# Attention heads in a new order of steps, and the differential layer's weight panels split by ScalarE and VectorE

## The chip, the cores and the metric

The kernel runs on one core of a Trainium2 chip. The metric is the time of one execution in microseconds (us), the median of three runs. TensorE (PE in the rows) multiplies, VectorE (DVE) reduces and works by element, ScalarE (ACT) evaluates functions and copies, GpSimd (POOL) works by element too, and SyncE (SP) issues most of the DMAs. The engines run side by side, each through its own list in order, and meet at semaphores.

## The reference, cut to what matters

One step of a trunk of four layers over 128 context tokens and 512 latent tokens (T = 640) of width 1024. Each layer is a modulated norm, a token mixer, a residual, a modulated norm, a SwiGLU FFN and a residual. The mixers are latent attention (MLA), differential attention, grouped-query attention with rotary positions, and a gated recurrence. The change touches the three attention mixers, of 8 heads each:

```python
def blocked_attention(q, k, v):          # per block of 128 queries
    sc = einsum('bqhgd,bkhd->bhgqk', qblk, k) * scale
    p = softmax(sc, axis=-1)
    return einsum('bhgqk,bkhd->bqhgd', p, v)

# differential: two softmaxes of 64-wide halves of q and k, one value
o = o1 - lam_full * o2
o = rmsnorm(o, g_sub) * (1.0 - lambda_init)
```

The query and the key of a head are projections of the layer's input, normed by their root mean square over the head's width and, for latent tokens, turned by rotary angles. In MLA a key is 128 values of its own beside 64 rotary values that all heads share (`kr`). In the differential layer they are 128 wide, two components of 64.

## The kernel before, in words

Everything lies transposed in SBUF: features on partitions, tokens along the free axis. A projection multiplies a 128-column panel of weights with all 640 tokens. To keep float32's precision each operand is split in a high and a low part, and `products` sums three products (high with high, high with low, low with high) over the panel's 8 tiles of 128 rows: 48 matmuls of 320 columns. Splitting a panel is two instructions over 128x1024: `w_hi` is a rounded copy of `raw`, `w_lo` is the difference. In the dense phases (output projections and FFN) ScalarE makes `w_hi` (`high_part`) and VectorE `w_lo` (`low_part`); in all others, the heads' projections among them, GpSimd does both. SyncE loads `raw` into three slots.

A head has two streams of work. The attention of head h goes over t = 0 to 4, blocks of 128 queries (4 of latent, 1 of context): scores (TensorE, float32 matmuls into banks psA and psB in turn), maximum (VectorE, L414, L418), exponential (ScalarE, L376), division (VectorE, `probs`, L422 to L429), five 128x128 transposes through psC (TensorE, L353, `turned`), a copy out of psC (ScalarE, L383, L385, `pt`), and at the end one product with the values (`pe_output`, L361). The preparation of head h + 1 is its projections into psD, evacuation (`evq`, `evk`: L395, L396), the sum of squares over partitions by a matmul with a matrix of ones (`ssq`, `ssk`: L312), the reciprocal root by a logarithm and an exponential (`rsq`, `rsk`: L400, L402), the norm (L434), a rotation by a matmul (`rotq`, `rotk`: L966, L976), the rotary sum (L438 to L441), and the transposes of the values. In the lists a step of the one stream stands between steps of the other. These orders are written out by hand in `head`, once for each of the three engines, and semaphores count marks in the same order (`pipelined_names` and the lists handed to `pipeline`). A list entry that waits holds up all behind it on its engine.

All preparation steps of one head, sums, rotations and value transposes included, use the one psum pair psD, so a projection cannot start before the last of them has been read. In the differential layer GpSimd splits three panels a head.

## Time and profile before

| | us |
|---|---|
| median of 3 runs (lowest, highest) | 3837.23 (3836.21, 3839.26) |
| the profiled execution | 3834.61 |
| its span | 3832.8 |
| TensorE busy in the span | 3417.5 (89%) |
| VectorE, ScalarE, GpSimd busy | 1907.0, 1093.3, 325.1 |
| granted TensorE clock, mean | 0.940 of full |

The chain of work that ended last is TensorE's for 78% of the span, ScalarE's for 8%, VectorE's for 6%. A timeline row gives the start, the length from the first start to the last end of a run of like instructions, and in brackets how long the engine sat idle before it and whose result ended the wait. TensorE's matmuls overlap: in a stream of 320-column products two start every 0.29 us though each row ends later, so lengths on TensorE are read from start to start. Full clock is 1.0.

### The profile page before, as it was taken

Reading aid. Unit: us, or ns where it says so; the run is one execution under the profiler, and the core shown is the slowest. Engines: PE = TensorE matmul, PEld = TensorE weight load, DVE = VectorE, ACT = ScalarE, POOL = GpSimd, SP = SyncE. Lnnn points to the kernel's source line nnn. Section 1 sums busy time; section 2 is a strip of 40 time slices with the busy share of each in tenths; the row PEclk is TensorE's granted clock in tenths of the full one; section 3 lists DMA queues with packets and bytes.
Section 4 is the critical chain, followed back from the end, with each engine's and each line's share of the span. In section 5 each row is a group of like instructions: output and inputs, shape, how many; then the busy total and the mean of one; then the engine's idle time right before and its main releaser. Section 6 shows DMA issues by size and latency. Waiting matters only on the chain.

```text
span 3832.8 us, 53039 instructions
## 1 busy us (share of the span) xinstructions
PE 3417.5 (89%) x20320; PEld 3050.3 (80%) x20320; DVE 1907.0 (50%) x2703; ACT 1093.3 (29%) x1710; POOL 325.1 (8%) x168
## 2 busy tenths in 40 slices
PE   7868888999987887789999878889999877799999
PEld 2645568999975666579999866589999877799999
DVE  2133345857353444458583534458573678633332
ACT  1324433211122333332111133332111255331111
POOL 0311100000012222000000021000000144000000
PEclk9979999999987888789999989999999988899999
DMA  7200003443221101025342210034442211122222
GB/s 264 90 14 12 17 23 112 147 156 123 75 69 32 32 27 32 3 76 182 124 155 72 71 38 18 17 99 159 137 143 71 66 52 41 55 66 77 72 76 77
DMA packets 421854, 304.02 MB, mean 79 GB/s; under 512 B 12019, under 2 KB 389494, under 8 KB 421622
## 3 DMA queue, kind: packets, MB, share of 16 engines
q1 hardware_dynamic: 411412, 293.23, 24.7%
q10 hardware_dynamic: 10338, 9.41, 0.7%
q8 instruction: 65, 1.06, 0.1%
q14 instruction: 39, 0.32, 0.0%
HBM read 298.49 MB, written 4.10 MB: 79 GB/s over the span
## 4 chain that ended last, share of the span: by engine, by line
PE 78%; ACT 8%; DVE 6%; DVEq 3%; issue 2%; ACTq 1%; DMA 1%; SPq 0%
PE psB L296 27%; PE psA L296 27%; PE psD L296 8%; PE psC L361 3%; PE psA L340 2%; PE psB L340 2%; ACT h_hi L1251 1%; PE psA L727 1%; ACT work L1248 1%; PE psD L312 1%; DVE work L2020 1%; PE psB L727 1%; PE psC L312 1%; ACT work L400 1%; ACT work L402 1%
## 5 line engine op out<-in xcount | busy, mean ns | idle before, releaser
L1269 ACT ACTIVATE w_hi<-raw 128x1024 fp32r<-128x1024 f32 (+1 forms) x304 | 314.2, 1035 | 1152.6 <-PE psB L296 762.1
L1734 DVE TENSOR_TENSOR w_lo<-raw,w_hi 128x1024 fp32r<-128x1024 f32 (+1 forms) x304 | 362.1, 1192 | 345.8 <-ACT w_hi L1269 345.4
L296 PE MATMUL psA<-h_hi,w_hi 128*128 128x320 f32 x1616 | 385.1, 320 | 71.8 <-DVE h_lo L1797 60.4
L697 POOL TENSOR_TENSOR w_hi<-raw,consts 128x1024 fp32r<-128x1024 f32 (+2 forms) x82 | 143.2, 1747 | 2916.1 <-PE psA L296 772.7
L296 PE MATMUL psA<-h_lo,w_hi 128*128 128x320 f32 x1616 | 377.0, 315 | 0.0
L296 PE MATMUL psA<-h_hi,w_lo 128*128 128x320 f32 x1616 | 376.6, 315 | 0.0
L296 PE MATMUL psB<-h_hi,w_hi 128*128 128x320 f32 x1616 | 368.7, 309 | 0.0
L296 PE MATMUL psB<-h_lo,w_hi 128*128 128x320 f32 x1616 | 368.6, 309 | 0.0
L296 PE MATMUL psB<-h_hi,w_lo 128*128 128x320 f32 x1616 | 368.6, 309 | 0.0
L296 PEld LDWEIGHTS psA<-h_hi,w_hi 128*128 128x128 f32 x1616 | 274.6, 193 | 92.2 <-issue 44.2
L1756 DVE SCALAR_TENSOR_TENSOR work<-work,silu_c 128x1024 f32<-128x1024 f32 x252 | 312.7, 1282 | 12.0 <-issue 0.5
L296 PEld LDWEIGHTS psA<-h_hi,w_lo 128*128 128x128 f32 x1616 | 278.6, 193 | 0.0
L296 PEld LDWEIGHTS psA<-h_lo,w_hi 128*128 128x128 f32 x1616 | 278.3, 193 | 0.0
L296 PEld LDWEIGHTS psB<-h_hi,w_hi 128*128 128x128 f32 x1616 | 270.8, 188 | 0.0
L296 PEld LDWEIGHTS psB<-h_lo,w_hi 128*128 128x128 f32 x1616 | 270.6, 188 | 0.0
L296 PEld LDWEIGHTS psB<-h_hi,w_lo 128*128 128x128 f32 x1616 | 270.4, 188 | 0.0
L296 PE MATMUL psA<-act_hi,w_hi 128*128 128x320 f32 x960 | 221.5, 312 | 18.4 <-DVE w_lo L1734 16.7
L296 PE MATMUL psA<-act_lo,w_hi 128*128 128x320 f32 x960 | 219.9, 310 | 0.0
L296 PE MATMUL psA<-act_hi,w_lo 128*128 128x320 f32 x960 | 219.8, 310 | 0.0
L296 PE MATMUL psD<-h_hi,w_hi 128*128 128x320 f32 (+1 forms) x672 | 181.1, 353 | 42.6 <-DVE work L441 15.6
L296 PE MATMUL psB<-act_hi,w_hi 128*128 128x320 f32 x960 | 218.8, 309 | 0.0
L296 PE MATMUL psB<-act_hi,w_lo 128*128 128x320 f32 x960 | 218.7, 309 | 0.0
(285 smaller groups left out, 5537.2 us busy)
## 6 DMA issues: line engine op xcount, KB each, us to landing
raw<-in_w_ffn_in SPq DMA_DIRECT2D x176, 512.0 KB, 3.9
work<-in_w_mod SPq DMA_DIRECT2D x144, 512.0 KB, 4.7
raw<-in_w_ffn_out SPq DMA_DIRECT2D x64, 512.0 KB, 3.7
work<-in_w_mod SPq DMA_DIRECT2D x12, 2048.0 KB, 8.1
raw<-in_w_ffn_out SPq DMA_DIRECT2D x32, 384.0 KB, 3.3
raw<-in_diff_w_in SPq DMA_DIRECT2D x24, 512.0 KB, 3.7
raw<-in_lru_w_in SPq DMA_DIRECT2D x16, 512.0 KB, 4.6
raw<-in_gqa_w_in SPq DMA_DIRECT2D x12, 512.0 KB, 3.7
```

Source lines behind the costliest of these rows:

```text
L296: last = nc.tensor.matmul(out[:, b, 0:half], w[slot][:, kt * cols + c0:kt * cols + c0 + P], r[:, o:o + half], start=(kt == 0 and p == 0), ...
L312: last = nc.tensor.matmul(out[:, b, 0:half], ones_, sq[:, b * half:(b + 1) * half], start=(k == 0), stop=(k == len(pieces) - 1))
L340: last = nc.tensor.matmul(s[:, b, 0:n], q[:, q0:q0 + P], k[:, k0:k0 + n], start=(m == 0), stop=(m == len(pairs[c]) - 1))
L361: nc.tensor.matmul(psC[:, 0, 0:NLAT], V[:, (k + 1) * P:(k + 2) * P], PT[:, k * NLAT:(k + 1) * NLAT], start=(k == 0), stop=(k == 4))
L400: nc.scalar.activation(halves(out, half), ps[:, :, 0:half], ACT.Ln, bias=eps, scale=1.0 / count)
L402: return nc.scalar.activation(out, out, ACT.Exp, scale=-0.5)
L697: nc.gpsimd.tensor_tensor(w_hi[s][:, 0:n], raw[s][:, 0:n], ones[:, 0:1].to_broadcast([P, n]), ALU.mult).then_inc(pool_hi, 1)
L727: last = nc.tensor.matmul(psum[q % 2][0:2, 0, :], silu_c[:, kt * 2:kt * 2 + 2], first_mod_w[q % 3][:, kt * 512:(kt + 1) * 512], start=(kt ...
L1248: nc.scalar.activation(s_, s_, ACT.Identity, bias=mod_col(layer, 3 * which, kt, cond), scale=gains[:, cond * KT + kt:cond * KT + kt + 1])
L1269: nc.scalar.activation(w_hi[s][:, 0:n], raw[s][:, 0:n], ACT.Copy).then_inc(hi_done, 1)
L1734: nc.vector.tensor_tensor(w_lo[s_][:, 0:n], raw[s_][:, 0:n], w_hi[s_][:, 0:n].bitcast(F32), ALU.subtract).then_inc(split_done, 1)
L1756: last = nc.vector.scalar_tensor_tensor(acc[cond], w_, c_, acc[cond], ALU.mult, ALU.add)
```

## The change

In all three attention mixers the hand-written lists are put in another order. In the two first mixers sums, rotations and value transposes go to psC, which the transposed probabilities use, and psD holds projections alone. A projection's 8 tiles are cut in pieces with steps of the attention between them, and waits are added so that psC's users follow one another. In the differential layer the end of a head (sum of squares of its output and its norm) moves into the next head. In MLA the rotary part of the score has all 128 rows (the shared key's first 64 are cleared, by one memset) instead of 64, and the loop over the two parts is outside the loop over banks. The maximum and the division of VectorE are separate steps, and the maxima come earlier. The differential layer becomes a dense phase for its panels: ScalarE makes `w_hi`, VectorE `w_lo`, two panels a head ahead for q and k and one head ahead for v, and those of its first head in the last turn of the FFN before it. GpSimd keeps the panels of MLA, grouped attention and the recurrence. The first two differential heads stand outside the loop.

The panel plan, the score loop, MLA's pairs, and TensorE's list of a differential head:

```diff
-            add("diff", HEADS, (2, 0, 1), [(KT, P)] * 3)
+            add("diff", HEADS, (2, 0, 1), [(KT, P)] * 3, True)
...
-                for b, k0, n in ((0, 128, TH), (1, 128 + TH, TH)) if t < 4 else ((0, 0, P),):
-                    for m, (q, k) in enumerate(pairs[c]):
+                for m, (q, k) in enumerate(pairs[c]):
+                    for b, k0, n in ((0, 128, TH), (1, 128 + TH, TH)) if t < 4 else ((0, 0, P),):
                         last = nc.tensor.matmul(s[:, b, 0:n], q[:, q0:q0 + P], k[:, k0:k0 + n],
                                                 start=(m == 0), stop=(m == len(pairs[c]) - 1))
...
                     def pairs(h):
                         k = h.k % 2
-                        return [[(qn_t[k], kn_t[k]), (qr_t[k][64:P], kr_t[64:P])]]
-
-                    def first_scores(h):
-                        for t in range(2):
...
+                        return [[(qn_t[k], kn_t[k]), (qr_t[k], kr_t)]]
+
+                    def scores(h, t):
+                        if t == 0:
...
+                    def head(h, more, first=False):
+
+                        n = h.next()
+                        prep = (lambda step, *k: step(n, *k)) if more else (lambda step, *k: None)
+                        prep(gq, 0, 1)
+                        turned_v(h)
+                        prep(gq, 1, 4)
+                        acts.wait(pe, "v", h)
+                        pe_turned(pe, A, h, 0, d_probs)
+                        scores(h, 2)
+                        prep(gq, 4, 5)
+                        pe_turned(pe, A, h, 1, d_probs)
+                        prep(gq, 5, 8)
+                        A[1].wait(pe, "pt1", h)
+                        if not first:
+                            output_sum(h.last())
+                        scores(h, 3)
+                        prep(gk, 0, 1)
+                        DIF_NORM.wait(pe, "rso", h.last())
+                        prep(ssq)
+                        prep(gk, 1, 3)
+                        if more:
+                            acts.wait(pe, "rsq", n)
+                        pe_turned(pe, A, h, 2, d_probs)
+                        prep(gk, 3, 8)
+                        A[1].wait(pe, "pt2", h)
+                        prep(rotq)
+                        scores(h, 4)
+                        prep(gv, 0, 1)
+                        prep(ssk)
+                        prep(gv, 1, 3)
+                        if more:
+                            acts.wait(pe, "rsk", n)
+                        pe_turned(pe, A, h, 3, d_probs)
+                        prep(gv, 3, 5)
+                        A[1].wait(pe, "pt3", h)
+                        prep(rotk)
+                        prep(gv, 5, 7)
+                        prep(kturn)
+                        prep(gv, 7, 8)
+                        if more:
+                            acts.wait(pe, "kcache", n)
+                        pe_turned(pe, A, h, 4, d_probs)
+                        prep(scores, 0)
+                        pe_output(pe, A, pv, h, dV[h.k % 2], d_PT, d_PTp)
+                        prep(scores, 1)
```

ScalarE's list of a differential head, the old one left out:

```diff
+                    def head(h, more, first=False, later=True):
+                        n = h.next()
+                        prep = (lambda step, *k: step(n, *k)) if more else (lambda step, *k: None)
+                        prep(cached)
+                        if not first:
+                            prep(high, 2)
+                        values(h)
+                        exp(h, 1)
+                        pt(h, 0)
+                        exp(h, 2, 0)
+                        if first:
+                            prep(high, 2)
+                        pt(h, 1)
+                        exp(h, 2, 1)
+                        prep(evq)
+                        if not first:
+                            output_rstd(h.last())
+                        prep(rsq)
+                        exp(h, 3)
+                        if later:
+                            high(n.next(), 0)
+                        pt(h, 2)
+                        prep(evk)
+                        prep(rsk)
+                        exp(h, 4)
+                        if later:
+                            high(n.next(), 1)
+                        pt(h, 3)
+                        prep(kout)
+                        prep(kcache)
+                        pt(h, 4)
+                        prep(evv)
+                        prep(exp, 0)
+                        output(h)
```

VectorE's low part of a panel and its list:

```diff
+            def low_part_of_head(name, h, j):
+
+                ph = phases[name]
+                s_, n = ph.slots[j], ph.shape[j][0] * ph.shape[j][1]
+                dve.wait_ge(hi_done, h.at(ph.n, ph.dense_first + j + 1))
+                nc.vector.tensor_tensor(w_lo[s_][:, 0:n], raw[s_][:, 0:n], w_hi[s_][:, 0:n].bitcast(F32),
+                                        ALU.subtract).then_inc(split_done, 1)
+
...
+                    def head(h, more, first=False, later=True):
                         n = h.next()
-                        prep = (lambda step: step(n)) if more else (lambda step: None)
-                        dve_tile(dve, A, h, 2, 2, scale, d_probs, d_stats)
+                        prep = (lambda step, *k: step(n, *k)) if more else (lambda step, *k: None)
+                        largest(h, 1)
+                        probs(h, 1)
+                        largest(h, 2)
+                        prep(low, 2)
+                        probs(h, 2)
+                        largest(h, 3)
+                        if not first:
+                            output(h.last())
                         prep(q_normed)
-                        dve_tile(dve, A, h, 3, 2, scale, d_probs, d_stats)
+                        probs(h, 3)
+                        prep(q_roped)
+                        largest(h, 4)
+                        if later:
+                            low(n.next(), 0)
                         prep(k_normed)
-                        prep(q_roped)
-                        dve_tile(dve, A, h, 4, 2, scale, d_probs, d_stats)
+                        probs(h, 4)
+                        if later:
+                            low(n.next(), 1)
                         prep(k_roped)
-                        prep(first_tiles)
```

At the end of the FFN before, and the memset in MLA:

```diff
 
                 turns = phases[name].turns
                 with act.Fori(0, turns - 1) as i:
                     each(i, lambda j: high_part(name, i + 1, j))
                 each(turns - 1, lambda j: high_part(then, 0, j) if then else None)
+                if then == "diff":
+                    high_part(then, 0, 2)
 
...
+                    nc.vector.memset(kr_t[0:64, 0:T], 0.0)
```

Grouped attention takes `pe_scores(2)` ahead of `turned0`, a cut of its projection at 4 and 7 of 8 tiles instead of at 4, and `turned4` ahead of the rotation `q_turn`; VectorE takes the maxima of two blocks ahead of their divisions.

TensorE's list at the fourth block of a differential head before, where psD serves the rotation (`psD<-work,consts 128x512`, L966) and the value projection after it:

```order
L95 REGISTER_ALU [waits diff_att_dve]
L353 MATMUL psC<-consts,work 128x128 [waits diff_att_act]
L353 MATMUL psC<-consts,work 128x128 x4
L95 REGISTER_ALU
L95 REGISTER_ALU [waits diff_prep_act]
L966 MATMUL psD<-work,consts 128x512 [waits diff_prep_dve]
L340 MATMUL psA<-work 128x128 [waits diff_att_act]
L95 REGISTER_ALU
L340 MATMUL psB<-work 128x128 [waits diff_att_act]
L95 REGISTER_ALU
L941 REGISTER_ALU [waits diff_prep_dve]
L296 MATMUL psD<-h_hi,w_hi 128x320 [waits split_done]
```

And the like place now (L1007 the rotation has been moved ahead of the block's scores, L311 is the sum of squares of k):

```order
L1007 MATMUL psC<-work,consts 128x512 [waits diff_prep_dve,diff_att_act]
L339 MATMUL psA<-work 128x128 [waits diff_att_act]
L339 MATMUL psB<-work 128x128 [waits diff_att_act]
L295 MATMUL psD<-h_hi,w_hi 128x320 [waits split_done,diff_prep_act]
L295 MATMUL psD<-h_hi,w_hi 128x320
L295 MATMUL psD<-h_lo,w_hi 128x320 x2
L295 MATMUL psD<-h_hi,w_lo 128x320 x2
L311 MATMUL psC<-work,consts 128x320 [waits diff_prep_dve,diff_prep_act]
L311 MATMUL psC<-work,consts 128x320
L295 MATMUL psD<-h_hi,w_hi 128x320 x2
L295 MATMUL psD<-h_lo,w_hi 128x320 x2
L295 MATMUL psD<-h_hi,w_lo 128x320 x2
```

The rotation stood behind two waits of the preparation and the value projection behind one more; now the value projection's first tile runs ahead of the sum, which is in psC.

ScalarE's list between the third and the fourth block of a differential head now (L373 exponential, L1365 `w_hi` of a panel, L380 and L382 the copy of transposed probabilities, L392 and L393 evacuation of k):

```order
L373 ACTIVATE work<-psA,work 128x640 [waits diff_att_dve]
L95 REGISTER_ALU
L373 ACTIVATE work<-psB,work 128x640 [waits diff_att_dve]
L1363 REGISTER_ALU
L1365 ACTIVATE w_hi<-raw 128x1024 [waits gemm_done,raw_in2]
L380 ACTIVATE work<-psC 128x4x128 [waits diff_att_pe]
L382 ACTIVATE work<-psC 128x128
L1504 REGISTER_ALU
L392 ACTIVATE work<-psD 128x640 [waits gemm_done]
L393 ACTIVATE work<-psD 128x640
```

Before, no `w_hi` stood in ScalarE's list of this layer's heads; now one stands between the exponentials and the copy that the next transposes wait for, and its own waits are for a projection and a DMA (`raw_in2`).

## Rows read from the trace of the kernel before

**Rows 1.** stretches: latent heads, differential heads, grouped heads (length, busy of each engine, granted clock, DMA).

```profile
206.20:556.10 349.90, 299.10 (x1193) 188.29 (x1194) 113.67 (x238) 139.67 (x274) 34.02 (x28) 0.94 0.05 16
...
1125.40:1624.90 499.50, 396.17 (x1884) 305.57 (x1884) 210.81 (x417) 178.46 (x399) 92.29 (x42) 0.84 0.09 26
...
2261.50:2484.40 222.90, 187.52 (x841) 131.62 (x842) 97.26 (x222) 79.10 (x186) 25.48 (x12) 0.92 0.07 20
```

**Rows 2.** one differential head, the same view, same columns.

```profile
1238.20:1296.50 58.30, 47.26 (x238) 37.15 (x237) 25.36 (x51) 21.00 (x49) 13.27 (x6) 0.88 0.11 32
```

**Rows 3.** who TensorE waited for in the differential heads (total, times, longest).

```profile
PE psD L966 <- ACT work L402: 26.0, 8, 3.5
PE psA L340 <- ACT work L376: 18.8, 10, 2.4
```

**Rows 4.** timeline of TensorE in a differential head (start, length, instructions, idle before).

```profile
1257.42 0.53 PE L340 MATMUL psA<-work 64*128 64x320 f32 x1
...
1258.70 0.56 PE L296 MATMUL psD<-h_hi,w_hi 128*128 128x320 f32 x2
...
1265.84 0.71 PE L353 MATMUL psC<-consts,work 128*128 128x128 f32 x5
1267.39 1.34 PE L312 MATMUL psD<-work,consts 128*128 128x320 f32 x4 [0.84 <-ACT work L396]
...
1275.81 1.12 PE L966 MATMUL psD<-work,consts 128*128 128x512 f32 x2 [3.49 <-ACT work L402]
...
1279.16 0.90 PE L296 MATMUL psD<-h_hi,w_hi 128*128 128x320 f32 x2 [1.80 <-DVE work L441]
```

**Rows 5.** one line's instructions: shortest/median/longest ns, first and last start.

```profile
L1427 ACTq DMA_DIRECT2D out_new_diff_k<-work x8: 350/362/373, 1180.5 to 1588.7; - x8
```

**Rows 6.** timeline of TensorE in a latent head.

```profile
276.03 1.56 PE L312 MATMUL psD<-work,consts 128*128 128x384 f32 x4 [1.74 <-ACT work L402]
...
301.83 2.90 PE L340 MATMUL psB<-work 128*128 128x320 f32 x8
304.66 0.62 PE L296 MATMUL psD<-h_hi,w_hi 128*128 128x384 f32 x2
...
316.26 1.56 PE L312 MATMUL psD<-work,consts 128*128 128x384 f32 x4 [1.74 <-ACT work L402]
```

**Rows 7.** timeline of ScalarE in a latent head: one reciprocal root, two instructions.

```profile
317.85 0.90 ACT L400 ACTIVATE work<-psD,small 128x768 f32<-128x768 f32 x1 [0.99 <-PE psD L312]
318.82 0.84 ACT L402 ACTIVATE work<-work 128x768 f32<-128x768 f32 x1
```

**Rows 8.** timeline of TensorE in the grouped heads.

```profile
2301.39 6.25 PE L361 MATMUL psC<-work 128*128 128x512 f32 x10 [0.37 <-ACT work L387]
...
2307.70 1.24 PE L340 MATMUL psB<-work 128*128 128x320 f32 x4
2308.78 1.24 PE L340 MATMUL psA<-work 128*128 128x320 f32 x4
...
2327.72 4.56 PE L361 MATMUL psC<-work 128*128 128x512 f32 x10 [0.37 <-ACT work L387]
```

**Rows 9.** ScalarE's and VectorE's groups by form: panel halves.

```profile
L1269 ACT ACTIVATE w_hi<-raw 128x1024 fp32r<-128x1024 f32 x272 | 287.2, 1057 | 1023.8 <-PE psB L296 686.3 <-PE psA L296 318.1 <-DMA raw<-in_w_ffn_in 19.4
...
L1734 DVE TENSOR_TENSOR w_lo<-raw,w_hi 128x1024 fp32r<-128x1024 f32 x272 | 331.7, 1221 | 326.5 <-ACT w_hi L1269 326.0 <-issue 0.2
```

**Rows 10.** timeline of all engines while GpSimd splits a panel.

```profile
1232.49 2.35 POOL L700 TENSOR_TENSOR w_lo<-raw,w_hi 128x1024 fp32r<-128x1024 f32 x1
...
1233.26 2.12 DVE L439 TENSOR_TENSOR work<-work,tables 128x512 f32<-128x512 f32 x1
```

**Rows 11.** timeline of VectorE, rotation of one head's query.

```profile
1276.97 0.69 DVE L438 TENSOR_TENSOR work<-psD,tables 128x512 f32<-128x512 f32 x1
...
1278.33 0.69 DVE L441 TENSOR_TENSOR work<-work 128x512 f32<-128x512 f32 x1
```

**Rows 12.** DMA issues of the differential layer (KB each, us to landing).

```profile
raw<-in_diff_w_in SPq DMA_DIRECT2D x18, 512.0 KB, 3.7
```

More of the change, by code:

```diff
@@ L889, in turned_v, with gkn @@
-                    def turned_v(h):
-                        dves.wait(pe, "qroped", h)
+                        pes.mark(sum_rows(psC, blocks, [sq_r], TH), "ssqr")
+                    def gkn(h, part):
+                        if part[0] == 0:
+                            pe.wait_ge(split_done, phases["mla"].of_head(h, 1, 2))
+                            acts.wait(pe, "evqr", h)
+                        last = ukv(h, 0, part)
+                        if part[-1] == 1:
+                            pes.mark(last, "gkn")
@@ new lines, in rotqr @@
+                    def rotqr(h):
+                        acts.wait(pe, "rsqr", h)
+                        dves.wait(pe, "qr", h)
+                        pes.mark(nc.tensor.matmul(psC[:, 0, 0:NLAT], rot64, qr_t[h.k % 2][:, NCTX:T],
+                                                  start=True, stop=True), "rotqr")
+                    def sskn(h):
+                        acts.wait(pe, "evkn", h)
+                        dves.wait(pe, "qroped", h)
+                        pes.mark(sum_rows(psC, ones, [sq_k], NKEY // 2), "sskn")
@@ L1026, in _ @@
+                    acts.wait(pe, "kcache", h0)
+                    scores(h0, 0)
+                    scores(h0, 1)
+                    head(h0, True, True)
+                    head(Head(0, 1), True)
+                    with pe.Fori(1, HEADS // 2 - 1) as i:
                         for k in range(2):
@@ L1470, in _ @@
+                    h0 = Head(0, 0)
+                    for step in (cached, evq, rsq, evk, rsk, kout, kcache):
+                        step(h0)
+                    high(Head(0, 1), 0)
+                    high(Head(0, 1), 1)
+                    evv(h0)
+                    exp(h0, 0)
+                    head(h0, True, True)
+                    head(Head(0, 1), True)
+                    with act.Fori(1, HEADS // 2 - 1) as i:
                         for k in range(2):
@@ L1963, in _ @@
-                    with dve.Fori(0, HEADS // 2 - 1) as i:
+                        prep(largest, 0)
+                        prep(probs, 0)
+                    h0 = Head(0, 0)
+                    for step in (q_normed, q_roped, k_normed, k_roped):
+                        step(h0)
+                    low(Head(0, 1), 0)
+                    low(Head(0, 1), 1)
+                    largest(h0, 0)
+                    probs(h0, 0)
+                    head(h0, True, True)
+                    head(Head(0, 1), True)
```

477 lines of the change are left out of this document (259 added, 218 removed).

## The prediction

> **What bounds the kernel now.** I read the stretches first. The three attention layers' heads take 349.9, 499.5 and 222.9 us, 1072 of 3832.8 [rows 1]; the code of the rest doesn't change. In the heads TensorE is busy 299.1, 396.2 and 187.5 us, at a granted clock of 0.94, 0.84 and 0.92 of full: 2.4 GHz with parts at 1.2. No other engine comes near: in a differential head of 58.3 us VectorE is busy 25.4 and ScalarE 21.0 [rows 2]. TensorE waits for results of the preparation's own chain. Its two costliest waits in the differential heads are for a reciprocal root ahead of the rotation (26.0 us, up to 3.5 a head) and for an exponential ahead of the second block's scores (18.8) [rows 3]. The timeline shows what follows such waits: behind the idle stretches of 3.49 and 1.80 us two products of the value projection take 0.90 us, where two after scores at full clock take 0.56 [rows 4]. So a removed wait also gives clock back.
>
> **Differential heads.** A head repeats every 58.3 us ((1588.7 - 1180.5) / 7) [rows 5]. TensorE's own work in one, at full clock, from start to start: three projections of 7.04 (1258.70 to 1265.84 is 7.14 with the change from scores), scores 4 x 1.28 and 0.42 for the context block, transposes 4 x 0.62 and 0.22, three sums of about 1.2, two rotations of 1.0, one output of 4.6, value and key transposes 0.7: 40.2 us [rows 4, 8]. The other 18.1 are waits (13 when I walk the three lists of before with these lengths) and half clock (5).
>
> The change removes and adds no matmul here, it moves them. I walked the new lists in the same way, each instruction starting when its engine is free and its waits are met, with 0.045 us from an end to the start that it releases. A head then takes 42.3 us, of which TensorE waits 2.1:
> - The sum of k's squares waits for the roped q: 0.17 (tail of the rotation) + 2.06 (three rotary instructions, 1276.97 to 1278.33 + 0.69 [rows 11]) + 0.09 = 2.32, less the context block's scores 0.42, one tile of the value projection 0.88 and 0.19 of another wait that it overlaps: 0.84 is left.
> - The transpose of the cached key waits for the roped k: 2.32 less two tiles (1.76): 0.56.
> - Value transposes for the output's evacuation (1.4 long), 0.4; for reciprocal roots and evacuations 0.1 to 0.2, together 0.4.
>
> The panels: ScalarE gets 3 x 1.06 us a head, VectorE 3 x 1.22 [rows 9]. With them ScalarE has 24 and VectorE 28 busy of 42 us, after VectorE gets back what it now loses beside GpSimd: a rotary product takes 2.12 us while GpSimd splits, the like ones 0.69 [rows 10, 11]. All work on panels is covered, as the walk places it: `w_hi` of slot 2 stands ahead of the copy of the third block's probabilities, and the next user of that copy is 4.4 us of k's projection away. Without that cover it would cost its 1.06. The first head's panels come in the FFN's last turn, ahead of a norm in which VectorE waits for ScalarE's root anyway; I cost them at nothing, at most 2 x 1.2.
>
> I add 0.7 a head for what the walk smooths (twelve pieces of projection in place of three, the change between 64-row and 128-row matmuls once more): 43.0. Six full periods: 6 x (58.3 - 43.0) = 92. First head with its preparation, and the last: 499.5 - 6 x 58.3 = 149.7 before. The walk gives 76.5 + 27.3, the norm's pace (the first projection follows the norm tile by tile) 7.3 as before, half clock in preparation and last head 13 (before 16.7: 149.7 less 125.7 walked and 7.3), mixing 0.7: 124.8. That is 25 saved. **Differential layer: -117.**
>
> **Latent heads.** Here a matmul gets cheaper. Eight score matmuls, alternating 128 and 64 rows, take 2.83 us (301.83 to 304.66), 0.354 each [rows 6]; the grouped layer's four of 128 rows, the same bank loop, take 1.08, 0.270 each [rows 8]. I take 2.2 for a block now. Bounds: 2.16, and no change at 2.83. The nearest row by shape is the lower, as all 128 rows are now used and the part is the outer loop. That is 4 x 0.63 + 0.25 = 2.8 a head. By the Trainium skill (TensorEngine Tiling, Key Properties) a change of tiling mode drains TensorE, which fits the row. But TensorE: Matmul & The Clock Gate, LDWEIGHTS, says that loading weights takes the same time whatever the rows, so padding alone would give nothing: by it the layer saves 13 in place of 33.
>
> Waits change little, 5.7 to 4.5 a head in the walks. The new ones are fixed by lengths: k's sum waits 1.84 for the roped q (2.32 less 0.48), the transposes of block 2 wait 0.96 for k's root (1.81 from 317.85 to 319.66 [rows 7], + 0.25, less half a projection of 1.10), those of block 3 0.97 for a copy, block 1 0.75 for a root. The period goes from 40.2 (316.26 - 276.03 [rows 6]; the walk of before gives the same) to 36.2. These waits stand close together, 3.8 us idle of 6.9. In the grouped layer a like crowding (3.4 of 5.2 in the walk of before) is followed by output products of 6.25 us in place of 4.56 [rows 8], in five heads of eight; in the latent heads of before (3.6 of 8.8) it never was. I take half of the heads, 0.9 each, and 0.3 for mixing: 37.4, so 6 x 2.8 = 17. First and last: 349.9 - 6 x 40.2 = 108.7, against 65.8 + 15.1 walked, 0.6 for the memset, which nothing covers, and 11 for half clock: 92.5. **Latent layer: -33.**
>
> **Grouped heads.** The walks give 24.7 and 23.6: the second block's copy is no longer waited for (0.56), nor is the output's; the waits of 1.5 for block 3's division and 1.0 for its copy are crowded, so that all eight heads may fall to half clock, not five: 9 - 3 = **-6**. The added wait for `qroped` before a projection is met already, since the first scores wait for it.
>
> **Sum.** 117 + 33 + 6 = 156. Against the profiled execution (3834.6; its span 3832.8 plus 1.8 around it, which stay) that is 3679; the median of before is 2.6 above that execution, so **3681**.
>
> **Rivals.**
> 1. *The latent scores don't get cheaper.* For it: no row shows two 128-row parts in one block, and the multiplications with zeros are new. Against: the grouped layer's rows. Price 2.5 to 2.8 in each of eight heads, 20: 3701.
> 2. *Waits stay in the differential heads.* The walk has slacks of a few tenths: the last head's root must be read out of psC before q's sum, and the copy of block 1 before the output's sum, both on ScalarE's list of 24 entries a head. If ScalarE and VectorE are 10% slower than in my lengths the walk gives 43.8, at 20% 46.1. With dips to half clock of 1.7 to 5 a head as before, heads of 46 to 49: 8 x 3 to 6, that is 3705 to 3729. For it: psC now serves five users in turn, each handed on by a wait. Against: no crowded idle stretch is left in the walk, 2.1 of 42.3, and the latent heads of before kept full clock with 5.7 of 40.2.
> 3. *VectorE beside GpSimd in the latent and grouped heads.* GpSimd stays there, and VectorE's instructions move. If one a head falls on it at 1.4 us (2.12 - 0.69) [rows 10, 11] on the path: 16 x 1.4 = 22: 3703. By the walk GpSimd runs right behind its projection, when VectorE reads psum, so I doubt it. The Trainium skill has the rule (SBUF — State Buffer, Who interferes with whom): a VectorE instruction with two SBUF inputs and a GpSimd one exclude each other for their whole length. By that rule, the trace agrees.
> 4. *Slower than before.* A panel comes late: `w_hi` waits for a DMA at the head of ScalarE's list, with exponentials and copies behind it and TensorE behind those. It decides when a differential head takes 156 / 8 = 19.5 us more than I reckon. A panel lands 3.7 us after issue [rows 12] and its slot is free a head (42 us) ahead, so it needs DMA to be ten times slower: over 3840.
>
> **How the numbers follow.** My forecast (3655 to 3698) 0.62; rivals 1 and 3 together 0.15; rival 2 0.19; the fourth, or a change that does nothing since a wait I didn't see replaces these, 0.04. Low end: no dips in latent heads (-7), no mixing (-8), preparation at full clock (-10), so 3656. High end: rivals 1 to 3 in part, 3722. What a measurement of this kernel can tell from no change is about 0.2%, 8 us; only the last case is near it. Faster 0.96, same 0.02, slower 0.02.
>
> **What would show each step.** Right: differential heads every 43 us, clock over 0.95 in six of them, no GpSimd work there, the largest wait under 1 us; ScalarE under 60% busy. Latent heads every 37, score blocks of 2.2. Grouped heads every 24. The clock of the whole near 0.95. Wrong: a wait for ScalarE's list ahead of a transposition or sum in every differential head; score blocks of 2.8; GpSimd beside a long rotary product; a longer FFN turn or norm ahead of the differential layer.

## The result, and the profile after

The changed kernel takes **3648.4 us** (median of 4 runs, 3643.6 to 3655.3), the kernel before 3836.7 beside it: a ratio of 0.951 (95% interval 0.9494 to 0.9526). The forecast was 3681 with a range of 3656 to 3722. The direction and the way it is saved were as forecast; the saving was 188 us in place of 156, which puts the time below the range, and the part that was off is the half clock. The profiled execution took 3648.95, its span 3646.3, 186.5 less than that of before; the granted clock of the whole is 0.959 (0.940 before).

The same three stretches as in [rows 1] (latent, differential, grouped heads: length, busy of PE, PEld, DVE, ACT, POOL, granted clock, DMA):

```profile
206.60:508.50 301.90, 262.34 (x1193) 194.32 (x1193) 111.94 (x238) 140.15 (x274) 34.04 (x28) 0.96 0.06 17
1074.00:1449.40 375.40, 348.79 (x1884) 269.52 (x1884) 221.69 (x438) 196.00 (x420) 0.00 (x0) 0.95 0.12 34
2083.81:2295.60 211.79, 180.66 (x840) 131.57 (x841) 98.86 (x222) 79.83 (x186) 25.45 (x12) 0.93 0.07 21
```

A head's period is read from the starts of two output products (L358), as six periods between the first and the seventh head. What is left of a stretch, ahead of the first output product and behind the seventh, is "first and last".

| us | before | forecast | after | saved | forecast saving |
|---|---|---|---|---|---|
| latent: one of six periods | 40.24 | 37.4 | 36.15 | 24.6 in six | 17 |
| latent: first and last | 108.4 | 92.5 | 85.0 | 23.4 | 16 |
| differential: one of six periods | 58.06 | 43.0 | 42.71 | 92.1 in six | 92 |
| differential: first and last | 151.1 | 124.8 | 119.2 | 31.9 | 25 |
| grouped: whole stretch | 222.9 | 216.9 | 211.8 | 11.1 | 6 |
| all the rest | 2760.5 | 2760.5 | 2757.2 | 3.3 | 0 |

The differential heads came out close to the walk. Who TensorE waited for in six of them, where [rows 3] has waits of 26.0 and 18.8 over the layer (total, times, longest):

```profile
PE psC L311 <- DVE work L443: 2.7, 6, 0.6
PE psC L1024 <- DVE work L443: 2.5, 6, 0.5
PE psD L295 <- ACT work L393: 0.7, 4, 0.2
```

And TensorE's timeline in one of them, to be set beside [rows 4], where the rotation waited 3.49 and the value projection 1.80:

```profile
1227.19 1.02 PE L1007 MATMUL psC<-work,consts 128*128 128x512 f32 x2
...
1228.81 0.55 PE L295 MATMUL psD<-h_hi,w_hi 128*128 128x320 f32 x2 [0.18 <-ACT work L393]
...
1230.35 1.34 PE L311 MATMUL psC<-work,consts 128*128 128x320 f32 x4 [0.40 <-DVE work L443]
...
1239.18 0.33 PE L1024 MATMUL psC<-consts,work 128*128 128x128 f32 x1 [0.40 <-DVE work L443]
```

The three waits that the prediction named are there, on the roped q (L311), the roped k (L1024) and the evacuation, 1.0 us a head together, where the walk had 2.1. The six periods as a window (columns as above, with a clock of 1.00, that is 2.4 GHz throughout; before, it was 0.88 in a head, [rows 2]):

```profile
1156.30:1412.50 256.20, 248.96 (x1418) 195.32 (x1416) 161.43 (x322) 139.30 (x304) 0.00 (x0) 1.00 0.13 37
```

TensorE's timeline in a latent head, to be set beside [rows 6]:

```profile
313.54 2.32 PE L339 MATMUL psA<-work 128*128 128x320 f32 x8
315.69 0.71 PE L350 MATMUL psC<-consts,work 128*128 128x128 f32 x5
...
325.22 0.74 PE L350 MATMUL psC<-consts,work 128*128 128x128 f32 x5 [0.83 <-ACT work L399]
...
330.16 1.56 PE L311 MATMUL psC<-work,consts 128*128 128x384 f32 x4 [1.71 <-DVE work L443]
...
333.80 0.74 PE L350 MATMUL psC<-consts,work 128*128 128x128 f32 x5 [1.04 <-ACT work L399]
...
335.40 0.77 PE L350 MATMUL psC<-consts,work 128*128 128x128 f32 x5 [0.85 <-ACT work L382]
```

A score block takes 2.15 from start to start (313.54 to 315.69) where it took 2.83, and the four waits, walked as 0.75, 1.84, 0.96 and 0.97, are 0.83, 1.71, 1.04 and 0.85. Yet this head takes 35.98, not 37.4: no half clock follows these waits here, and of the six periods one only is longer (37.34). Here the forecast begins to fail.

### The profile page after: what moved, and what is told of

It is laid out like the page before. It is cut to its first block, busy times and chain, and to the rows that moved or that the text cites. A ratio compares the mean times of both kernels' runs of the same rounds, so it can differ in the third digit from the quotient of the medians.

```text
span 3646.3 us, 53064 instructions
## 1 busy us (share of the span) xinstructions
PE 3323.3 (91%) x20320; PEld 3018.5 (83%) x20320; DVE 1915.9 (53%) x2728; ACT 1115.1 (31%) x1734; POOL 217.2 (6%) x120
## 4 chain that ended last, share of the span: by engine, by line
PE 81%; DVE 6%; ACT 6%; DVEq 2%; issue 2%; ACTq 1%; DMA 1%; SPq 0%
PE psB L295 29%; PE psA L295 29%; PE psD L295 7%; PE psC L358 3%; PE psA L339 2%; PE psC L311 2%; PE psC L350 2%; PE psB L339 2%; ACT h_hi L1339 1%; PE psA L729 1%; ACT work L1336 1%; DVE work L2216 1%; PE psB L729 1%; ACTq L1338 1%; ACT work L397 1%
## 5 line engine op out<-in xcount | busy, mean ns | idle before, releaser
L699 POOL TENSOR_TENSOR w_hi<-raw,consts 128x1024 fp32r<-128x1024 f32 (+2 forms) x58 | 93.6, 1614 | 2840.8 <-PE psA L295 1675.6
L295 PE MATMUL psA<-act_hi,w_hi 128*128 128x320 f32 x960 | 221.6, 312 | 18.4 <-DVE w_lo L1870 16.7
L295 PE MATMUL psB<-act_lo,w_hi 128*128 128x320 f32 x960 | 218.7, 309 | 0.0
```

The source lines that it names most:

```text
L295: last = nc.tensor.matmul(out[:, b, 0:half], w[slot][:, kt * cols + c0:kt * cols + c0 + P], r[:, o:o + half], start=(kt == 0 and p == 0), ...
L699: nc.gpsimd.tensor_tensor(w_hi[s][:, 0:n], raw[s][:, 0:n], ones[:, 0:1].to_broadcast([P, n]), ALU.mult).then_inc(pool_hi, 1)
```

## Experiments

"The changed kernel" is 3648.4, and 3650.9 in a second series (run after_again). Stretch lengths and periods are read from each run's own trace as above.

**The latent score block.** Two things changed in it at once, the rows and the loop order. These edits of the changed kernel take them back:

```diff
-                        return [[(qn_t[k], kn_t[k]), (qr_t[k], kr_t)]]
+                        return [[(qn_t[k], kn_t[k]), (qr_t[k][64:P], kr_t[64:P])]]
```
```diff
-                for m, (q, k) in enumerate(pairs[c]):
-                    for b, k0, n in ((0, 128, TH), (1, 128 + TH, TH)) if t < 4 else ((0, 0, P),):
+                for b, k0, n in ((0, 128, TH), (1, 128 + TH, TH)) if t < 4 else ((0, 0, P),):
+                    for m, (q, k) in enumerate(pairs[c]):
```

Both taken back (scores_old), the rows alone taken back (scores_64_parts_outside), the loop order alone taken back (scores_128_banks_outside), and, in the kernel before, only the new block with its memset and all orders old (before_scores_new):

> The changed kernel with the latent layer's score blocks as before: 64 rotary rows, and the loop over the two parts inside the one over banks. All orders of steps stay new. Theory 1, that the score matmuls and the order each gave their share: a block of four float32 products takes 2.83 us again in place of 2.15, a latent head 38.7 in place of 36.0 (walked), the latent stretch grows from 301.9 to about 323, the whole by 21 to about 3669. Rival, that the new order alone lets TensorE run ahead and the blocks are hidden: under 8 us in all.

> The changed kernel with 64 rotary rows, but the loop over the two parts outside: one turn from 128 to 64 rows and one back in a block, where the old loop has four such turns. Theory 1, that each turn between 128 and 64 rows costs (2.83 - 2.15) / 4 = 0.17: a block takes 2.49, a head 37.3, the whole about +10 to the changed kernel. Rival a, that a matmul of 64 rows is slow by itself: 2.83, +21. Rival b, that the loop order alone counts: 2.15, +0.

> The changed kernel with all 128 rotary rows, but the loop over banks outside again. Theory 1, that turns between row counts cost: there are none, a block takes 2.15 and nothing changes, within 3 us of the changed kernel. Rival, that leaving a bank after each product or changing the weights more often is what costs: 2.83 a block, +21.

> The kernel before, with only the latent score blocks changed: 128 rotary rows, the first 64 of the shared key cleared, parts outside. All orders stay old. Theory 1, that it is a saving of TensorE's own work that carries over to any order: blocks of 2.15, a latent head 37.8 in place of 40.2 (walked: TensorE's waits grow from 5.7 to 6.0 a head), the latent stretch 19 us shorter, the whole about 3818. Rival, that in the old order the waits eat it since TensorE waits on the preparation's chain: under 8 us saved.

| run | turns between 128 and 64 rows a block | block | latent period | latent stretch | median |
|---|---|---|---|---|---|
| changed kernel | 0 | 2.15 | 36.15 | 301.9 | 3648.4 |
| scores_128_banks_outside | 0 | 2.16 | 36.61 | 303.7 | 3650.4 |
| scores_64_parts_outside | 2 | 2.44 | 37.72 | 314.3 | 3664.1 |
| scores_old | 4 | 2.83 | 39.66 | 325.8 | 3672.6 |
| before_scores_new | 0 | 2.16 | 37.58 | 323.0 | 3811.0 |

The blocks in the timelines of scores_old, scores_64_parts_outside and scores_128_banks_outside, each with the instruction behind it:

```profile
428.38 2.90 PE L339 MATMUL psA<-work 128*128 128x320 f32 x8
431.21 4.56 PE L358 MATMUL psC<-work 128*128 128x512 f32 x10
```
```profile
420.22 2.51 PE L339 MATMUL psA<-work 128*128 128x320 f32 x8
422.66 4.56 PE L358 MATMUL psC<-work 128*128 128x512 f32 x10
```
```profile
414.22 2.32 PE L339 MATMUL psA<-work 128*128 128x320 f32 x8
416.38 4.46 PE L358 MATMUL psC<-work 128*128 128x512 f32 x10
```

A turn is a change from 128-row to 64-row matmuls or back. It is the turns that cost, 0.14 to 0.17 us each, not the 64 rows and not the loop order: with no turn in it the block takes 2.16 in either order. Both rivals of the second run (2.83, 2.15) fell, and 2.44 is near the 2.49 of theory 1. The whole kernels lost somewhat more than was expected of their blocks (24 for 21 in scores_old, 16 for 10 in scores_64_parts_outside); each has at least one period that is 1.3 longer than its neighbours.

The saving belongs to TensorE's own work and carries over to the old order: 27 us of stretch (349.9 to 323.0), a ratio of 0.9935 (0.9916 to 0.9953). It was expected as 19; the first head gave 8.1 where the walk had 2.4. There TensorE was busy 51.25 us in place of 59.84 for the same 211 matmuls, at a clock of 0.86 in place of 0.78, and the cheaper blocks are 2.7 of that: the rest is clock. The new order of steps brings the other 21.

**The panels and the order, in the differential layer.** First the changed kernel with GpSimd splitting again (diff_gpsimd), then the kernel before with only the panels moved to ScalarE and VectorE (before_panels). The core of the two edits, the list entries left out:

```diff
-            add("diff", HEADS, (2, 0, 1), [(KT, P)] * 3, True)
+            add("diff", HEADS, (2, 0, 1), [(KT, P)] * 3)
```
```diff
-            add("diff", HEADS, (2, 0, 1), [(KT, P)] * 3)
+            add("diff", HEADS, (2, 0, 1), [(KT, P)] * 3, True)
...
                         act_exp(act, A, h, 1, 2, scale, d_probs, d_stats)
+                        if more:
+                            high(n, 2)
...
                         prep(rsk)
+                        if later:
+                            high(n.next(), 0)
```

> The changed kernel with the differential layer's panels on GpSimd again, as before; the new order of its steps stays. Theory 1, that the order of the steps is what saves and the panels' engine hardly matters: heads of at most 43.5 in place of 42.7, the layer at most +8; ahead of the layer's norm the wait of 3.0 for the squares is 6.7 again as in the kernel before (+3.7), so about 3655 to 3660. Rival, that GpSimd beside VectorE is a large part: GpSimd splits 12.8 us of each head, VectorE stands 59% of a head, so up to 7 us of its work is drawn out and TensorE's waits for the roped q and k grow: heads of 45 to 48, +20 to +45, and the clock below 0.95 in them.

> The kernel before, old orders everywhere, with the differential layer's panels split by ScalarE and VectorE (w_hi of v behind the second block's exponentials, of q and k behind the reciprocal roots; w_lo at like places). Theory 1, that the long waits come from the order (psD handed from step to step): the heads stay at 58 within 1, the wait ahead of the norm falls from 6.7 to 3.0, so 3.7 and a few us more, about 3825 to 3835. Rival, that the panels alone free VectorE enough: heads of 55 or less, under 3810.

| | panels by GpSimd | panels by ScalarE and VectorE |
|---|---|---|
| old order: period, stretch | 58.06, 499.5 | 59.57, 506.1 |
| new order: period, stretch | 46.38, 400.2 | 42.71, 375.4 |

As whole kernels, before_panels has a ratio of 1.0002 (0.999 to 1.0014), no change; diff_gpsimd takes 3683.4, 35 more than the changed kernel. Theory 1 was wrong for diff_gpsimd, and its rival, heads of 45 to 48, came true: in the new order the panels' engine is worth 3.7 us a head. For before_panels theory 1 held in that the long waits come from the order, but its numbers did not: the heads went from 58.1 to 59.6 where they were to stay within 1, and the whole took 3838 where 3825 to 3835 was expected.

The place in diff_gpsimd is one (all engines of diff_gpsimd, around the rotation of q):

```profile
1243.39 1.02 DVE L441 TENSOR_TENSOR work<-work,tables 128x512 f32<-128x512 f32 x1
1243.94 2.67 POOL L702 TENSOR_TENSOR w_lo<-raw,w_hi 128x1024 fp32r<-128x1024 f32 x1
1244.49 2.67 DVE L443 TENSOR_TENSOR work<-work 128x512 f32<-128x512 f32 x1
...
1247.21 2.50 PE L311 MATMUL psC<-work,consts 128*128 128x320 f32 x4 [2.72 <-DVE work L443]
```

The same instruction in the changed kernel, and the waits of six heads in diff_gpsimd:

```profile
1229.61 0.69 DVE L443 TENSOR_TENSOR work<-work 128x512 f32<-128x512 f32 x1
```
```profile
PE psC L311 <- DVE work L443: 14.3, 6, 2.9
PE psC L1024 <- DVE work L443: 2.5, 6, 0.5
```

The last addition of the rotary sum takes 2.67 in place of 0.69 while GpSimd's `w_lo` runs, and TensorE waits 14.3 in place of 2.7 for it: 1.9 a head. The rest, 1.8, is TensorE busy longer with the same matmuls (260.0 in place of 249.0 in six heads): clock, 0.95 in place of 1.00. By the Trainium skill (SBUF — State Buffer, Who interferes with whom) such a pair of instructions shares an exclusive port; the trace agrees. In the old order freeing VectorE brings nothing: the two longest waits are for ScalarE and stay as they were to the tenth (six heads of before_panels; the kernel before has the same two lines),

```profile
PE psD L966 <- ACT work L402: 20.8, 6, 3.5
PE psA L340 <- ACT work L376: 11.8, 6, 2.0
```

TensorE is idle 65.7 us in place of 65.9 over six heads, and busy 291.7 in place of 282.5, at a clock of 0.86 in place of 0.88. Why the clock is lower there, with the panels in ScalarE's and VectorE's lists, was not tried apart. So the panels' half of the change pays in the new order only; the order alone, with GpSimd, already brings a head from 58.1 to 46.4.

**The cut of the projections.** The changed kernel with the projections of a differential head in one piece each (diff_uncut); so for q, and alike for k and v:

```diff
-                        prep(gq, 0, 1)
+                        prep(gq, 0, 8)
                         turned_v(h)
-                        prep(gq, 1, 4)
                         acts.wait(pe, "v", h)
                         pe_turned(pe, A, h, 0, d_probs)
                         scores(h, 2)
-                        prep(gq, 4, 5)
                         pe_turned(pe, A, h, 1, d_probs)
-                        prep(gq, 5, 8)
```

> The changed kernel with the three projections of a differential head in one piece each, at the place of their first piece; sums, rotations and transposes stay in psC and in the new order, the panels with ScalarE and VectorE. Theory 1, that the cut of the projections is what fills the waits: walked, TensorE waits 16.4 us a head (for q's and k's roots and the copies behind them 1.7 to 2.6 each, for k's rotation 2.3) in place of 2.1, a head takes 56.6 at full clock in place of 42.3, and with 2 to 5 of half clock behind such waits 59 to 61, the whole about 3760 to 3790. Rival, that freeing psD of the sums is the main part and TensorE runs ahead without the cuts: heads under 48, the whole under 3690.

It takes 3805.1, a ratio of 0.9908 (0.9885 to 0.993); a head takes 64.08, 6 more than in the old order, and the whole lies above the 3760 to 3790 expected. (It is still 35 us below the kernel before, since the latent and grouped heads keep their new order.) The four costliest waits in six heads (total, times, longest), and the six heads as a window (start and end, length, TensorE busy, then the clock, 0.82):

```profile
PE psC L350 <- ACT work L399: 21.7, 12, 1.9
PE psC L1024 <- DVE work L443: 13.1, 6, 2.2
PE psC L1007 <- ACT work L382: 13.0, 6, 2.4
PE psC L1017 <- ACT work L382: 8.2, 6, 1.5
```
```profile
1178.88:1563.38 384.50, 307.55 (x1419) 0.82 0.09 25
```

The waits stand where the walk had them, for the roots, the copies and k's rotation. TensorE is idle 12.8 a head (walked 16.4) and busy 51.3, against 41.5 in the changed kernel with the same matmuls: the 9.8 between these is clock. By the walk, a head of 56.6 at full clock, the clock costs 7.5 where I gave 2 to 5; either way it is the clock that was taken too small. So the new order, its use of psC included, is a loss when each projection stands in one piece at the place of its first piece. Other places for an uncut projection were not tried.

**The clock behind crowded waits.** In the changed kernel, one or two useless copies ahead of k's reciprocal root in each latent head (mla_wait1, mla_wait2); the times hold that extra work:

```diff
                         pes.wait(act, "sskn", h)
+                        for t_ in (sq_r, sq_n)[:1]:
+                            nc.scalar.activation(t_, t_, ACT.Copy)
                         acts.mark(rstd(act, sq_k, psC, P, NKEY // 2), "rskn")
```

> The changed kernel with one copy of 128x640 on ScalarE (0.76 us, of no use) ahead of the reciprocal root of k in each latent head, so that TensorE's wait of 1.04 ahead of the third block's transposes grows to about 1.8. By the walk a head grows from 36.0 to 36.7. Theory 1, that crowded waits take the clock down: the projection and scores behind it run at half clock in all heads, as they do now in one or two, each then 36.7 + 1.4 = 38.1, the whole +13 to +18. Rival, that which head loses clock isn't decided by these waits: 1 to 3 heads of 8 as now, +6 to +8.

> The same with two copies (1.5 us): the wait grows to about 2.6, a head walked at full clock to 37.5. Theory 1: half clock behind it in all heads, 38.9 or more each, the whole +20 to +26. Rival: heads of 37.5 but one to three, +12 to +15.

| run | wait ahead of block 2 | walked at full clock | periods of the first six heads | median |
|---|---|---|---|---|
| changed kernel | 1.04 | 36.0 | 35.98 four times, 37.34, 35.63 | 3648.4 |
| mla_wait1 | 1.67 | 36.7 | 37.82, 37.69, 37.64, 39.26, 36.59, 36.25 | 3657.9 |
| mla_wait2 | 2.3 | 37.5 | 38.57, 39.89, 38.58, 39.91, 38.57, 38.07 | 3675.1 |

One head of mla_wait2 (start, length, what the idle time before ended):

```profile
303.56 0.74 PE L350 MATMUL psC<-consts,work 128*128 128x128 f32 x5 [2.28 <-ACT work L399]
305.15 1.16 PE L350 MATMUL psC<-consts,work 128*128 128x128 f32 x5 [0.85 <-ACT work L382]
305.96 0.99 PE L295 MATMUL psD<-h_hi,w_hi 128*128 128x384 f32 x2
```

Behind the second wait five transposes take 1.16 in place of 0.77, and two products of the projection behind them 0.99 in place of 0.62 [rows 6]. Of six periods one lies well above the walk in the changed kernel, four in mla_wait1, all in mla_wait2. In these six periods TensorE needs 190.5, 195.2 and 199.6 us busy for the same 895 matmuls, at a clock of 0.99, 0.96 and 0.94: it is not the waits alone that grow. Theory 1 holds for two copies (+24 to +27 us for 12 of added waiting) and half for one (+7 to +10 for 6, where 13 to 18 were expected): the loss sets in by and by.

**Two more panels, and a base.** after_again is the changed kernel; kv_dense gives the panels of the grouped layer's shared keys and values to ScalarE and VectorE too; better also moves two panels of the first differential preparation forward:

```diff
-            add("gqa_kv", 2, (0, 1), [(KT, P)] * 2)
+            add("gqa_kv", 2, (0, 1), [(KT, P)] * 2, True)
```
```diff
-                    for step in (cached, evq, rsq, evk, rsk, kout, kcache):
+                    for step in (cached, evq, rsq, evk):
                         step(h0)
                     high(Head(0, 1), 0)
+                    rsk(h0)
                     high(Head(0, 1), 1)
-                    evv(h0)
+                    for step in (kout, kcache, evv):
+                        step(h0)
```

> The changed kernel itself, once more, as the base of the two runs beside it: 3648 within 5. The latent stretch 301.9 with one head of six longer by 1.4; if which heads lose clock is a matter of chance, another number of them now.

> The changed kernel with the four panels of the grouped layer's shared keys and values split by ScalarE and VectorE too, the first two in the last turn of the FFN before, as the differential layer has them now. Theory 1, that GpSimd beside VectorE draws out the residual's squares there (0.82 us to 1.4 and 2.9) and so delays the norm: the wait of 5.7 ahead of the norm's sum falls to 3.0, -2.7 and a little more in the key's rotation, about 3645. Rival, that the two panels in ScalarE's and VectorE's lists take as long: no change.

> The same, and in the differential layer's first preparation the panels of the second head's q and k a few steps earlier (behind the evacuation of k and the root of k), so that they don't stand ahead of the first exponential. Theory 1: TensorE's wait of 3.5 us for the first exponential falls by up to 2, so 3643 to 3645, within what can be told of the run beside it. Rival: the rotation behind them comes later and nothing is saved.

Medians 3650.9, 3645.0 and 3646.2, ratios to the kernel before 0.9519 (0.9502 to 0.9536), 0.9517 (0.9502 to 0.9531) and 0.9506 (0.9486 to 0.9525). The waits move as expected, 5.7 to 3.0 ahead of the grouped layer's norm and 3.5 to 2.1 ahead of the first differential scores, 4 us together. That is less than these runs can tell, so neither is shown to be faster than the changed kernel. after_again was to show another number of longer latent heads if they are a matter of chance. It did not: the same one of the six periods is longer, 37.35, though its last latent head took 1.6 more and its grouped stretch 3.5 more than in the first trace.

## Why the prediction was right, and where its size was off

**Differential heads: right.** Six periods saved 92.1, forecast 92. (By output products the period before was 58.06 and not 58.3; that moves 1.4 between the periods and the first and last heads and leaves the sum as it is.) TensorE waits 1.0 a head (walked 2.1), and what I called mixing is more than the 0.7 I gave: 42.71 less 40.2 of own work and 1.0 of waits leaves 1.5. So the 43.0 is right partly because these two offset each other. ScalarE was 54% busy (139.3 of 256.2; the walk's 24 of 42 is 57%), GpSimd idle, the clock 1.00: all that the last part of the prediction asked for. The reasons were right too: diff_uncut shows that without the pieces between psC's users the order is no gain. But "all work on panels is covered" names only what the panels cost. What they give, 3.7 a head against the same order on GpSimd, was in the walk unpriced, since the walk took VectorE's lengths without GpSimd; no rival was built on it.

**Score block: right.** 2.15, forecast 2.2. The Trainium skill's rule on a change of tiling mode (TensorEngine Tiling (Array Packing), Key Properties) fits all four loops: the time goes by the number of turns. I had read the Trainium skill's rule on loading weights (TensorE: Matmul & The Clock Gate, LDWEIGHTS) as speaking against the padding. The trace of scores_old agrees with the rule itself: loading the weights of a score matmul took 184 ns with 64 rows and 189 to 194 with 128. Nothing against the padding followed from it.

**The step that failed is half clock.** In the prediction it stands as 13 in the differential first and last heads, 11 in the latent ones, 0.9 a head (as a mean over six heads) in the latent periods, and 3 more than before in the grouped heads, which makes 12.5 over their walk. I had taken what the kernel before lost, by its walk, and shortened it a little: 16.7 to 13, 13.6 to 11. Length, busy TensorE and clock of first and last heads, before and then after (latent first, latent last, differential first, differential last; then DMA; the other engines are left out):

```profile
206.20:283.86 77.66, 59.84 (x211) 0.78 0.04 12
...
525.32:556.10 30.78, 27.45 (x89) 0.89 0.11 32
1125.40:1233.15 107.75, 81.51 (x378) 0.79 0.10 29
...
1581.53:1624.90 43.37, 32.16 (x91) 0.69 0.01 4
```
```profile
206.60:270.41 63.81, 53.50 (x233) 0.88 0.07 18
...
487.30:508.50 21.20, 18.31 (x67) 0.92 0.10 30
1074.00:1156.28 82.28, 72.47 (x386) 0.91 0.13 38
...
1412.52:1449.40 36.88, 27.33 (x84) 0.72 0.02 4
```

The order of steps fills the first preparation as it fills a full head (some matmuls of the last head's window now stand in the first one's): TensorE is busy 84% of the latent one and 88% of the differential one (77% and 76% before), and the clock rises with it, 0.78 to 0.88 and 0.79 to 0.91. A figure that needs no walk: over first and last head together, the latent ones keep TensorE busy 15.5 us less, of which the cheaper score blocks are 5.4, and the differential ones 13.9 less with the same matmuls. Idle time is not in these figures.

Taken as stretch less walk, half clock cost 3.5 in the latent first and last heads (85.0 - 80.9 - 0.6) in place of 11, and 8.1 in the differential ones (119.2 - 103.8 - 7.3) in place of 13. In the last differential head, which has no preparation to fill it, the clock stayed low, 0.72. Six latent periods lost 1.4 to it in place of 5.4; the 0.3 a head for mixing wasn't there either. The grouped stretch lost 7.4 over its walk of 204.4 (by hand, as all walked figures are; no run shows it): three output products of eight are over 5 us long (6.39, 5.13 and 7.29), not all eight, and some 2 of the 7.4 are not clock but rival 3 (below).

The profiled sum was off by 30.5. Of these, half clock has 4.9 in the differential layer, 7.5 and 4.0 in the latent one and 5.1 in the grouped one, 21.5 together; the rest is small: 3.5 of latent periods walked or padded too long (36.2 and 0.3 for mixing), 2.4 in the differential heads (42.71 for 43.0, no mixing in the first and last), and the 3.3 that follow (the parts are rounded).

**The rest was costed at nothing and gave 3.3.** It lies ahead of the differential layer, where the way from the latent heads' end to the layer's first projection went from 569.3 to 565.5; the other parts cancel within 0.5. All engines at the end of the FFN, before:

```profile
1106.42 2.42 POOL L700 TENSOR_TENSOR w_lo<-raw,w_hi 128x1024 fp32r<-128x1024 f32 x1
1106.65 2.87 DVE L1653 TENSOR_TENSOR work<-x 128x640 f32<-128x640 f32 x1
...
1109.59 2.36 DVE L1655 TENSOR_TENSOR work<-work 128x640 f32<-128x640 f32 x1
...
1117.32 2.50 PE L312 MATMUL psC<-work,consts 128*128 128x320 f32 x4 [6.66 <-DVE work L1655]
```

and after:

```profile
1058.91 0.82 DVE L1789 TENSOR_TENSOR work<-x 128x640 f32<-128x640 f32 x1
1059.81 0.82 DVE L1791 TENSOR_TENSOR work<-work 128x640 f32<-128x640 f32 x1
...
1065.96 2.50 PE L311 MATMUL psC<-work,consts 128*128 128x320 f32 x4 [3.04 <-DVE work L1791]
```

I asked what the first panels cost ScalarE and VectorE in the FFN's last turn, at most 2.4, and not what GpSimd had cost VectorE at the same place: squares of 0.82 us took up to 2.87. Both runs that move the differential layer's panels show it: the wait is 6.6 again in diff_gpsimd and 3.0 in before_panels.

**The rivals.** Rival 1 fell by the blocks, rival 2 by the waits of 0.6 at most. Rival 4 did not occur. Rival 3 fell in the latent heads: their waits are the walked ones, and the addition of the rotary sum took 0.69 in all 35 places of the changed kernel. In the grouped heads it came true in small. A division (L427), the one that the transposes of block 3 wait for, falls on GpSimd's `w_lo` in five of eight heads:

```profile
2140.55 2.35 POOL L702 TENSOR_TENSOR w_lo<-raw,w_hi 128x1024 fp32r<-128x1024 f32 x1
2142.21 1.05 DVE L427 TENSOR_SCALAR work<-work 128x640 f32<-128x640 f32 x1
2143.31 0.77 PE L350 MATMUL psC<-consts,work 128*128 128x128 f32 x5 [1.85 <-DVE work L427]
```

It takes 1.05 in place of 0.55, and TensorE waits 1.85 in these heads, 1.32 and 1.36 in the next two. I had walked 1.5. That is 0.5 in each of five heads, 2.5 us; before, the longest division there took 0.85, so part of this is old.

What was missing is a rival on the other side: that waits removed give back more clock than is counted. With the latent heads at their walk, preparation at full clock and the grouped heads at theirs, the same working gives 3681 less some 40. The range's low end took 25 off, of which 17 are clock.

**Open.** Which latent or grouped heads drop to half clock isn't explained: the same lists with the same waits do not give the same number in every trace (below). How the loss in the first and last heads divides between clock and the rest goes by the walk; no run tries these heads by themselves. Single parts of the grouped layer's new order were not tried, so its 11 us are read from the trace alone.

## What to carry to other kernels

When an order of steps removes waits, reckon the clock of the new schedule from the new schedule's own idle time, the first and last heads too, and not as the old loss less a little; and give the range a case in which nearly all of it comes back. Moving the small users from one psum pair to another paid here only with pieces of a long projection between them: the same order uncut had longer heads than the old one. Moving work off GpSimd is worth what the VectorE instructions beside it lose on the path, so it gave nothing in the old order, 3.7 us a head in the new one, and 3.6 once ahead of a norm; look for the same collision in the layers where GpSimd stays. Two parts of a product that differ in rows are best padded, or at least not alternated.

## What the runs showed of the hardware

- Turning between 128-row and 64-row float32 matmuls cost 0.14 to 0.17 us each; matmuls of 64 rows were not slower by themselves, nor was loading their weights (184 ns beside 189 to 194).
- A VectorE division of 0.55 us took 1.05 beside GpSimd's `w_lo`, an addition of 0.69 took 2.67, a square of 0.82 took 2.87.
- Which heads fall to half clock changes from trace to trace without a change in their lists. In seven traces in which the latent heads differ at most in the order of two loops (the changed kernel, after_again, kv_dense, diff_gpsimd, better, diff_uncut, scores_128_banks_outside), 1, 1, 1, 2, 2, 3 and 3 of six periods were 1.4 us longer. It need not be chance: the two traces of the changed kernel have the same period longer, diff_gpsimd and better share their two, diff_uncut and scores_128_banks_outside share their three. The grouped stretch, its heads' lists the same, took 208.4 to 208.6, 211.7 to 212.0 or 215.3 to 215.5, and here the two traces of the changed kernel differ (211.8 and 215.3). This may be part of why the changed kernel's runs spread over 3640 to 3655; two of its nine runs have traces, so it is not shown.
